# Attention with output products one more head behind: the two attentions unrolled, the end of each reordered

## The reference, cut to what matters

```python
c_act = silu(c)
mod = c_act @ ada_w[i] + ada_b[i]                 # 1024 x 6144 weights per layer
sh_a, sc_a, g_a, sh_f, sc_f, g_f = split(mod, 6)
h = rms_norm(x, norm_g[i, 0]) * (1 + sc_a) + sh_a
y = attention(h, w_qkv[i], w_o[i], ...)
x = x + g_a * rms_norm(y, norm_g[i, 1])
h = rms_norm(x, norm_g[i, 2]) * (1 + sc_f) + sh_f
x = x + g_f * rms_norm(swiglu(h, ffn_w_in[i], ffn_w_out[i]), norm_g[i, 3])
```

## Time and profile before

| | us |
|---|---|
| median of 3 runs (lowest, highest) | 1054.37 (1051.28, 1055.65) |
| span of the profiled execution, first to last instruction | 1056.5 |
| first attention, from PE's first product to the last of w_o | 40.12 to 154.89 |
| second attention, the same | 371.50 to 498.01 |
| PE / DVE / ACT busy, share of the span | 93% / 81% / 51% |
| mean granted TensorE clock | 0.953 of full |

### The profile page before, as it was taken

The page is one execution under the profiler, slowest core; times in us unless marked ns, Lnnn a source line. Parts: engine busy times, 40 slices in busy tenths (PEclk is TensorE's granted clock), DMA queues, the critical chain, the costliest instruction groups (busy, mean ns, idle before and its releaser), DMA issues.

```text
span 1056.5 us, 19816 instructions
## 1 busy us (share of the span) xinstructions
PE 981.8 (93%) x6740; PEld 902.7 (85%) x6740; DVE 853.2 (81%) x1354; ACT 543.3 (51%) x1013; POOL 68.9 (7%) x114
## 2 busy tenths in 40 slices
PE   3899997999999998998799999989998989999997
PEld 2899976999999787996699999979996789999995
DVE  6779987888878786776888878879998789987875
ACT  2464444444444464664444444449997455555542
POOL 3100012000000201112200000020000010000001
PEclk9999996999999898998799999989998979999999
DMA  9999971999999766561299999993230448666540
GB/s 339 325 329 321 327 228 49 338 315 313 306 307 319 221 198 177 158 203 40 62 338 315 307 309 315 311 281 108 81 120 0 129 132 280 215 185 190 181 120 40
DMA packets 259077, 233.39 MB, mean 221 GB/s; under 512 B 7513, under 2 KB 208986, under 8 KB 259034
## 3 DMA queue, kind: packets, MB, share of 16 engines
q1 hardware_dynamic: 256256, 226.52, 70.4%
q0 software_dynamic: 1536, 4.81, 1.4%
q10 hardware_dynamic: 1242, 1.51, 0.4%
HBM read 231.75 MB, written 1.06 MB: 220 GB/s over the span
## 4 chain that ended last, share of the span: by engine, by line
PE 78%; DVE 11%; issue 4%; ACT 3%; DMA 2%; POOL 1%; DVEq 0%; POOLq 0%; ACTq 0%
PE work L474 45%; PE Y L487 23%; PE work L647 4%; DVE mix L1506 2%; DVE wlo L1129 2%; PE work L536 1%; DVE xs L1177 1%; DMA ada_raw<-in_ada_w 1%; PE Y L750 1%; DVE acc L1141 1%; POOL small L428 1%; DVE mix L1232 1%; PE Y L547 1%; ACT whi L835 1%; ACT xs L923 1%
## 5 line engine op out<-in xcount | busy, mean ns | idle before, releaser
L1129 DVE TENSOR_TENSOR wlo<-raw,whi 128x1024 fp32r<-128x1024 f32 x286 | 347.0, 1221 | 95.2 <-ACT whi L835 94.2
L474 PE MATMUL work<-h_hi,whi 128*128 128x256 f32 x1440 | 410.0, 285 | 11.7 <-DVE h_lo L1189 11.7
L474 PE MATMUL work<-h_lo,whi 128*128 128x256 f32 x1440 | 407.0, 283 | 0.0
L474 PE MATMUL work<-h_hi,wlo 128*128 128x256 f32 x1440 | 407.0, 283 | 0.0
L835 ACT ACTIVATE whi<-raw 128x1024 fp32r<-128x1024 f32 x286 | 298.4, 1055 | 135.9 <-PE work L474 66.9
L474 PEld LDWEIGHTS work<-h_hi,whi 128*128 128x128 f32 x1440 | 276.0, 192 | 17.0 <-issue 13.7
L474 PEld LDWEIGHTS work<-h_lo,whi 128*128 128x128 f32 x1440 | 275.6, 191 | 3.1
L474 PEld LDWEIGHTS work<-h_hi,wlo 128*128 128x128 f32 x1440 | 276.1, 192 | 0.0
L1141 DVE SCALAR_TENSOR_TENSOR acc<-ada_raw,csil,acc 128x512 f32 (+1 forms) x256 | 191.0, 746 | 4.0 <-DMA ada_raw<-in_ada_w 1.7
L487 PE MATMUL Y<-whi,ab_hi 128*128 128x512 f32 x328 | 107.8, 410 | 1.9 <-DVE ab_lo L1249 1.9
L487 PE MATMUL Y<-wlo,ab_hi 128*128 128x512 f32 x328 | 105.2, 402 | 0.0
(11 more groups left out here) (187 smaller groups left out, 1162.8 us busy)
## 6 DMA issues: line engine op xcount, KB each, us to landing
ada_raw<-in_ada_w SPq DMA_DIRECT2D x88, 512.0 KB, 6.8
raw<-in_ffn_w_in SPq DMA_DIRECT2D x88, 512.0 KB, 7.2
ada_raw<-in_mod_w SPq DMA_DIRECT2D x48, 512.0 KB, 6.4
raw<-in_ffn_w_out SPq DMA_DIRECT2D x44, 512.0 KB, 5.2
raw<-in_f_up_w SPq DMA_DIRECT2D x44, 512.0 KB, 4.1
raw<-in_moba_w_qkv SPq DMA_DIRECT2D x24, 512.0 KB, 7.3
raw<-in_diff_w_qkv SPq DMA_DIRECT2D x24, 512.0 KB, 4.9
raw<-in_a_pw_w SPq DMA_DIRECT2D x24, 512.0 KB, 5.1
```

Of the source, the lines that this page charges most:

```text
L474: mm = pe.matmul(dst, w[:, u, ws], h[:, k, :], start=(k == 0 and m == 0), stop=(k == KT - 1 and m == 2))
L1129: dve.tensor_tensor(wlo[:, u, :], raw[:, u, :], whi[:, u, :].bitcast(F32), ALU.subtract).then_inc(lo[u], 1)
```

## The change

SP, PE, ACT and DVE's loops over the attention's steps are unrolled. SP's order of loads stays as it was. The rest, cut to its core:

```diff
 # PE, step n
-                    if j:
-                        head_values(i, 0)
-                    elif not start:
-                        head_values(i - 1, 1)
-                    if not start:
-                        w_o(i - 1, j, first=isinstance(i, int) and i == 1 and j == 0)
+                    if s == 0 and n > 2:
+                        w_o((n - 3) // 2, 1 - j, first=n == 3)
+                    if n:
+                        head_values((n - 1) // 2, 1 - j)
+                    if s == 2 and n > 2:
+                        w_o((n - 3) // 2, 1 - j, first=n == 3)
                     if j == 0:
                         values(T, i + nb)
 # PE, after step 7
+                w_o(NI_A - 2, 1)
                 if s == 0:
+                    probs_T(T - 1, more=False)
+                    w_o(NI_A - 1, 0)
+                    head_values(NI_A - 1, 1)
+                    pe.wait_ge(sb_done, H)
                     pe.wait_ge(v_ev, NI_A)
-                mod_gate_a(s // 2)
-                if s == 2:
+                    mod_gate_a(0)
+                else:
                     head_out_T(T - 2, T // 2)
-                probs_T(T - 1, more=False)
-                head_values(NI_A - 1, 1)
-                w_o(NI_A - 1, 0, half_way=(lambda: head_out_T(T - 1, T // 2)) if s == 2 else None)
+                    probs_T(T - 1, more=False)
+                    pe.wait_ge(sb_done, 2 * H + HEADS[2])
+                    pe.wait_ge(gemv, 8 * (NBLK + 6))
+                    mod_gate_half(2 * D, GATE_BANK[2], 0)
+                    head_values(NI_A - 1, 1)
+                    mod_gate_half(2 * D, GATE_BANK[2], 1).then_inc(mod_ga, 1)
+                    w_o(NI_A - 1, 0, half_way=lambda: head_out_T(T - 1, T // 2))
                 w_o(NI_A - 1, 1, end=True)
 # ACT, step n (last: n == 7)
-                    if more:
+                    if not last:
                         prep(j, i + (nb + 1))
                         prep(2 + j, i + (nb + 1))
 ...
-                    prep(6 + j, i + nb3)
+                    if n:
+                        if s == 2:
+                            squares(T - 1)
+                        else:
+                            out_hi((n - 1) // 2, 1 - j)
+                        prep(7 - j, (n - 1) // 2 + nb3)
 # ACT, after step 7
                 probs_T(T - 1)
+                prep(7, NI_A - 1 + nb3)
                 if s == 2:
                     squares(T - 1)
+                    prep(1, NI_A + nb)
                 out_hi(NI_A - 1, 1)
+                if s == 0:
+                    prep(1, NI_A + nb)
+                prep(3, NI_A + nb)
+                prep(5, NI_A + nb)
 # DVE, step n
                     softmax(T, n, between)
-                    if s == 2 and not first:
-                        norm_out(T - 1)
-                    prep(6 + j, i + nb3)
-                    sums(4 if s == 0 else 0, 8)
-                    if more:
+                    if n:
+                        if s == 2:
+                            norm_out(T - 1)
+                        else:
+                            out_lo((n - 1) // 2, 1 - j)
+                        prep(7 - j, (n - 1) // 2 + nb3)
+                    if s == 2:
+                        gemv_step(1, NBLK - 3, n)
+                    elif not last:
+                        sums(4, 8)
+                    if not last:
                         prep(4 + j, i + (nb + 1))
 # DVE, after step 7
-                gate_a(s)
+                prep(7, NI_A - 1 + nb3)
                 if s == 2:
                     copy_out(T - 1)
+                    prep(1, NI_A + nb)
                     norm_out(T - 1)
-                out_lo(NI_A - 1, 1)
+                    out_lo(NI_A - 1, 1)
+                    gate_a(2)
+                else:
+                    out_lo(NI_A - 1, 1)
+                    gate_a(0)
+                    for q in range(4, 8):
+                        gemv_step(0, H + 1, q)
+                    prep(1, NI_A + nb)
+                prep(3, NI_A + nb)
+                prep(5, NI_A + nb)
```

More of the change, by code:

```diff
@@ L505, in mod_first, with mod_gate_half @@
                 mod_columns(2 * layer, layer, 0)
+            def mod_gate_half(base, bank, f):
+                return pe.matmul(work[:, bank + f, :], ones[:], acc[:, base + f * BLK:base + (f + 1) * BLK],
+                                 start=True, stop=True)
             def mod_gate(base, bank, done):
[L509 to L512, removed]
+                mod_gate_half(base, bank, 0)
+                mod_gate_half(base, bank, 1).then_inc(done, 1)
             def mod_gate_a(layer):
@@ L951, in squares, with step @@
                                        scale=0.125, accum_out=sso[:, t:t + 1]).then_inc(oss, 1)
[L953 to L956, removed]
+                def step(i, j):
+                    n = i * 2 + j
+                    T = n + hb
+                    last = n == H - 1
                     act.wait_ge(used[j], i + (nb + 1))
@@ L997, in attention @@
                     act.wait_ge(lam_seq, 5)
-                sweep(act, 1, NI_A, s, both)
+                for i in range(NI_A):
+                    step(i, 0)
+                    step(i, 1)
                 T = hb + H
@@ L1301, in softmax, with step @@
                                                  pr[:, 1, a:b], ALU.mult, ALU.subtract).then_inc(p_done, 1)
[L1303 to L1306, removed]
+                def step(i, j):
+                    n = i * 2 + j
+                    T = n + hb
+                    last = n == H - 1
                     def sums(q0, q1):
-                        if s == 0 and not start:
+                        if i:
@@ L1310, in sums @@
                             for q in range(q0, q1):
[L1311 to L1314, removed]
+                                gemv_step(0, n + 2, q)
                     if s == 0:
                         sums(0, 4)
-                    if s == 2 and not start:
+                    elif n > 1:
                         out_lo(i - 1, j)
@@ L1321, in between @@
                     def between():
-                        if s == 2 and not first:
+                        if s == 2 and n:
                             copy_out(T - 1)
[L1325 to L1329, removed]
+                        if not last:
                             prep(j, i + (nb + 1))
                             prep(2 + j, i + (nb + 1))
-                    softmax(T, i * 2 + j, between)
@@ L1334, in step @@
-                    if s == 2 and not first:
-                        norm_out(T - 1)
-                    prep(6 + j, i + nb3)
-                    sums(4 if s == 0 else 0, 8)
-                    if more:
+                    softmax(T, n, between)
+                    if n:
+                        if s == 2:
[3 more added lines that the diff above has]
+                        prep(7 - j, (n - 1) // 2 + nb3)
@@ L1339, in step @@
+                    if s == 2:
+                        gemv_step(1, NBLK - 3, n)
+                    elif not last:
+                        sums(4, 8)
+                    if not last:
                         prep(4 + j, i + (nb + 1))
-                def both(i, more):
-                    step(i, 0, more)
-                    step(i, 1, more)
-                sweep(dve, 1, NI_A, s, both)
+                for i in range(NI_A):
+                    step(i, 0)
+                    step(i, 1)
```

35 lines of the change are left out of this document (9 added, 26 removed).

## The result

Median of 4 runs after: 1081.89 us (1080.12 to 1082.51); before, in the same comparison, 1054.26 (1051.28 to 1055.65). The ratio is 1.026, 95% interval 1.024 to 1.028: +27.6 us. The forecast was 1069 us, +14.6. The sign and the place of the loss are as forecast. The time is within the range by only 0.1 us, and the loss is nearly twice the predicted one. The profiled execution spans 1078.3 us, in a run of 1080.12.

The account below looks back on a forecast made before the run. In the first attention PE, DVE and transfers are all full; the second has transfer room and waits. First attention +19.4 us and second -5.2 gave +14.2, on the median of 1054.37 a forecast of 1069 us, range 1058 to 1082.

Parts of the forecast that it names:

- The mechanism: First attention: SP waits at the w_o load for the later `prep`, delaying v and quarters; DVE stalls six times, 2.6 us each.
- What I forecast for the trace: First attention: six `ada_raw` waits of 2 to 4 us, about 270 GB/s, softmaxes 15 to 16 us apart.
- The first attention's steps: Steps 2 to 7: +4.0 us, then +12.6 over five steps of 15.55; softmax 7 begins 16.6 us later.
- How long does the quarter take from the release?: First attention, w_o release to first quarter's landing: taken as 6.7 us, with 6.4 and 8.4 kept; DVE has 4.1 us cover.
- The sum of rates: First attention's burst: w_o lands after 3.2 us, v and quarter follow at 1.61 us each, 6.4 us in all.
- the slow burst of the earlier trace: Second attention before: first quarter landed 8.4 us after w_o's issue, some 1.1 us put down to a late unit in between.
- The first attention's end: After softmax 7: sums and `prep`s stand behind the last low part; post_norm at S + 17.7 for S + 14.2, net +2.8 us.
- The second attention: Gains 5.2 us: 3 around steps 0 to 2 from spread sums and the deferred product, 2.2 at its end.
- the v product starts at 404.0 instead of 411.1: Second attention, step 2 without w_o product: 7.1 us earlier, 2.8 of it coming back as the deferred product; 3 taken.
- The slow burst: Rival: first attention's quarters land after 8.4 us instead of 6.7, +10 us, 1079 up to 1083; chance 0.16.
- No stall: Rival: first attention's quarters land in time, DVE keeps 12.97 us a step; 1051 us, not slower; chance 0.09.
- With the end mended as well: Rival: no stall, first attention's end work hidden in PE's wait, second attention gains 6.5 us; 1045 us; chance 0.08.

Follow-up runs that it names:

- e2: Kernel before, with only the first attention's w_o-unit `prep` on ACT and DVE moved one step later, behind the next softmax: 1079.42 us, ratio 1.0245.
- e1: Kernel after, with SP's w_o load of the first attention issued behind v and the quarters: 1058.61 us, ratio 1.0054 to before.
- e10: Kernel before, with the first attention's w_o `prep` one step later and SP's w_o load behind the quarters: 1056.01 us, ratio 1.0012.
- e5: Kernel after with old second attention; first attention's w_o load behind the quarters, four last sums ahead of head 7's w_o `prep`: 1055.42 us, ratio 1.0011.
- e6: As e5, with the next stage's three `prep`s moved behind its pre_norm on ACT and DVE: 1052.17 us, ratio 0.9974 to before.
- e4: The change in the first attention alone, second attention as in the kernel before: 1082.06 us, ratio 1.0278.
- e3: The change in the second attention alone, first attention as in the kernel before (SP's load order the same): 1055.09 us, ratio 1.0012.
- e11: Kernel after, w_o load last and four sums earlier in the first attention, next stage's `prep`s behind its pre_norm in both: 1049.11 us, ratio 0.9943.
- e7: Kernel after, with SP issuing v alone ahead of the w_o load in the first attention: 1069.97 us, ratio 1.0128 to before.

## Why the prediction was half right

**The mechanism: right.** SP's order as the place, the w_o load standing for a `prep` now behind the softmax, v and the quarters behind it, six waits: e2 has them by that one `prep` (26.1 us, 6), e1 and e10 lose them by the order of loads alone. What I forecast for the trace is there, though three of the waits are over 4 us (6.60, 4.29, 4.16) and the rate fell to 250 GB/s, where I had forecast 270. PE's clock fell to 0.90 in the stretch, but the steps did not get longer by it: DVE's cycle in the rows above, 5.8 us to the release, 8.5 to the quarter and 3.1 to the next softmax, is the whole of the 17.4 us between its softmaxes. With the mean of 7.6 us it makes 16.5, and 16.57 are measured.

**The first attention's steps: a term mis-sized.** It is the step "How long does the quarter take from the release?". I took 6.7 us, between a sum of rates (6.4) and the one row of such a burst (8.4). Measured in the six steps: 7.64, 7.66, 8.42, 8.29, 6.73, 6.80, a mean of 7.6. Six times 0.9 is 5.4 us. The softmaxes are 16.57 us apart in five steps (15.55 forecast), and softmax 7 begins 22.8 us later (16.6 forecast). The sum of rates fails in its last term: v lands 1.3 to 1.7 us behind w_o, as the rate has it, but the first quarter 2.0 to 3.3 behind v. Between later quarters it is mostly 1.3 to 1.4. I set the slow burst of the earlier trace rows aside because its unit in between was released late. That unit did land late, 3.7 us behind w_o, and the quarter 1.5 behind it; in the first attention the long gap stands ahead of the third load in its place. It is not the quarters' own: in the second attention of the kernel after, five bursts go into an empty queue, four of them with a weight unit in third place, and the third load lands 6.9 to 8.2 us after w_o's issue. What makes the gap no run told.

The Trainium skill, DMA: Bandwidth & Descriptors, section Anatomy of one DMA, gave 5.6 us for the three by my estimate. The trace disagrees, at 6.7 to 8.4: the page's fit is per DMA (on the GpSimd path), and the w_o units, first in the burst, do agree with it (3.2 to 3.5 us, once 4.5).

**The first attention's end: right.** With S the start of softmax 7, post_norm comes at S + 18.1; the forecast was S + 17.7, and before it was S + 14.2. e5 and e6 show its two parts: without the `prep`s between gate and post_norm the stretch is 4.7 us shorter in the two profiles, the time 3.3 us. In sum the first attention took 25.9 us more in the profiles, forecast 19.4: 6.2 by the steps, 0.4 by the end. By the timed runs of e4 it is more, 29 us (1.0278).

**The second attention: wrong.** Forecast -5.2, measured +1.3 us, 1.0012 (0.9996 to 1.0027), in e3. Single times came out: post_norm at S + 18.7 for S + 19.3 (S here the start of the second attention's softmax 7), the wait of line 592 at 0.46 for 0.4. But two things failed. First, "the v product starts at 404.0 instead of 411.1" took away the w_o product without asking what it covered: the copy of head 1's output. The v product waits 1.7 us for it, and line 614 0.9 more than before. All of PE's waits in the second attention come to 10.3 us before and 8.7 after; the main ones before (371 to 504 us), beside those of after above:

```profile
PE work L591 <- DVE mix L1262: 5.1, 3, 2.7
PE work L613 <- DVE ab_lo L1251: 2.9, 2, 2.0
```

Second, the 5.2 was read off one execution, in which PE ran at a clock of 0.93 in that stretch. The same code, in e2:

```profile
398.00:520.00 122.00, 114.21 (x831) 102.14 (x830) 89.13 (x174) 70.55 (x176) 14.09 (x33) 0.96 0.55 163
```

It had 0.96 and took 133.8 us in place of 138.1, so a part of what I meant to gain is there or not from one execution to the next. Most of that difference is matmul time: from PE's first product to the end of the stretch PE is busy for 121.3 us before, and 118.0 to 118.6 us in e2, e4 and e5, with the same 860 matmul records. How much of the -5.2 each of the two took is open.

**The execution that was profiled.** The spans differ by 21.8 us and the medians by 27.6. In every run with both numbers time and span are 1.8 us apart; then the profiled execution of before took 1058.3, near the highest of its runs (1051.68 to 1058.5 in 23), and that of after the lowest of its four. I had set span and median 2.1 us apart and thought it harmless; it is 4.0 us by which that execution was slower than the median.

**The rivals.** The slow burst, at 1079 to 1083, was the nearest in time; it stood at 0.16. Its landing of 8.4 us was there in two of the six bursts alone (8.4 and 8.3). That the time still falls into the stated range is in part luck: the upper bound of 1082 was set for the slow burst, and what brought the time there was a burst mis-sized by 0.9 us a step and a gain that the second attention didn't give (14.6 + 6.2 + 0.4 for the first attention + 6.5 for the second make 27.7 us). No stall (1051) is the state that e1 makes of the kernel; it took 1058.6. With the end mended as well (1045) it is e11, at 1049.1.

## What to carry to other kernels

On a queue that issues in order, the release of a buffer is due not when its own transfer is needed but when the most urgent transfer behind it is: before a release is moved by a microsecond, list what stands behind the waiting load, or put the load last (22 us here, e1). Whoever takes a product out from between two waits has to ask what it covered. Here the next stage's preparations were better behind its norm than between a gate and the norm that waits for it (3.3 us, e6). And a gain of a few us that is read off one profiled execution wants the same code's other executions beside it: here they differ by 4 us.

## What the runs showed of the hardware

- Three loads of 512 KB issued together after an idle queue land 3.2 to 3.5 us (once 4.5), 4.7 to 6.0 us and 6.7 to 8.4 us after the first issue (the kernel after, six bursts). In e7, where the first quarter is second in the burst, it lands after 5.0 to 6.3 us.
- SP's issue of one load into an empty queue takes 0.34 us. In five of the six bursts of the kernel after, the eighth load, issued with six under way, held SP for 3.0 to 4.5 us (it is most of the 5.40 in the rows above). The number under way doesn't settle it alone: in the second attention the fourth of a burst, with three under way, took 1.9 to 2.0 us in three bursts and 0.5 in two. The cause stays open.
- The same code of the second attention took 133.8 to 138.1 us in six executions, with the granted clock at 0.96 in e2's and 0.93 in before's and e6's. PE has waits of 0.5 to 3 us in it in all of them.
